# Masking the diagonal blocks of eight forgetting heads on GpSimd instead of TensorE, and preparing the output weight in 32 pieces

## The reference, cut to what matters

```python
def fox_attend(q, k, v, cq, ck, q_pos, k_pos):
    s = jnp.einsum("bqhd,bkhd->bhqk", q, k) * (HEAD_DIM ** -0.5)
    bias = cq[:, :, :, None] - ck[:, :, None, :]        # c: running sum of log f
    mask = k_pos[None, :] <= q_pos[:, None]
    p = jax.nn.softmax(jnp.where(mask, s + bias, -jnp.inf), axis=-1)
    return jnp.einsum("bhqk,bkhd->bqhd", p, v)
# merge: the two normalised, gated groups side by side, times w_out
y = jnp.einsum("bte,ed->btd", jnp.concatenate([ya, yb], -1), w_out)
```

## Time and profile before

| what | value |
|---|---|
| median of 3 runs | 1066.63 us |
| the profiled execution's own time | 1068.08 us |
| its span | 1066.3 us |
| PE busy | 1017.2 us (95%) |
| DVE busy | 661.0 us (62%) |
| ACT busy | 463.4 us (43%) |
| POOL busy | 257.4 us (24%) |

### The profile page before, as it was taken

The page is one execution under the profiler, slowest core; times in us unless marked ns, Lnnn a source line. Parts: engine busy times, 40 slices in busy tenths (PEclk is TensorE's granted clock), DMA queues, the critical chain, the costliest instruction groups (busy, mean ns, idle before and its releaser), DMA issues.

```text
span 1066.3 us, 27354 instructions
## 1 busy us (share of the span) xinstructions
PE 1017.2 (95%) x11316; PEld 858.2 (80%) x11316; DVE 661.0 (62%) x979; ACT 463.4 (43%) x911; POOL 257.4 (24%) x198
## 2 busy tenths in 40 slices
PE   6899999999999999999999998999988999999997
PEld 5898778986778888888878987777766788887886
DVE  5557455654565546565645723676767877787487
ACT  5522312222021232232222323676687787787353
POOL 2300000000000010111201110400065566667596
PEclk9999999999999999999999999999998999999999
DMA  6366787798889787779878787855444452421343
GB/s 228 109 242 230 241 325 290 259 362 317 306 319 353 289 312 284 300 261 369 318 297 299 267 250 232 232 137 130 111 94 93 96 110 60 98 70 51 138 164 133
DMA packets 121328, 234.02 MB, mean 219 GB/s; under 512 B 60536, under 2 KB 91256, under 8 KB 103808
## 3 DMA queue, kind: packets, MB, share of 16 engines
q1 hardware_dynamic: 95872, 209.33, 58.1%
q10 hardware_dynamic: 25344, 23.08, 6.3%
HBM read 204.52 MB, written 27.86 MB: 218 GB/s over the span
## 4 chain that ended last, share of the span: by engine, by line
PE 80%; DVE 5%; issue 4%; ACT 4%; POOL 3%; DMA 2%; ACTq 1%; DVEq 0%; SPq 0%; POOLq 0%
PE bank L887 28%; PE bank L874 8%; PE bank L951 7%; PE bank L997 6%; PE bank L1246 6%; PE bank L1665 6%; PE bank L1222 5%; PE bank L1199 5%; PE bank L980 3%; DVE pr L1468 2%; PE bank L1261 1%; PE bank L1177 1%; DMA k_buf<-in_cache_sb_k 1%; PE bank L940 1%; POOL o_nat L1834 1%
## 5 line engine op out<-in xcount | busy, mean ns | idle before, releaser
L887 PE MATMUL bank<-w_hi,hT_hi 128*128 128x256 f32 (+1 forms) x896 | 260.7, 291 | 3.5 <-DVE hT_lo L620 3.1
L887 PE MATMUL bank<-w_lo,hT_hi 128*128 128x256 f32 (+1 forms) x896 | 253.2, 283 | 0.2 <-issue 0.2
L887 PE MATMUL bank<-w_hi,hT_lo 128*128 128x256 f32 (+1 forms) x896 | 252.9, 282 | 0.0
L887 PEld LDWEIGHTS bank<-w_hi,hT_hi 128*128 128x128 f32 x896 | 170.6, 190 | 11.1 <-issue 5.4
L887 PEld LDWEIGHTS bank<-w_lo,hT_hi 128*128 128x128 f32 x896 | 170.8, 191 | 0.5 <-issue 0.4
L887 PEld LDWEIGHTS bank<-w_hi,hT_lo 128*128 128x128 f32 x896 | 170.6, 190 | 0.0
L534 ACT ACTIVATE u_out<-bank 128x256 f32<-128x256 f32 x112 | 42.9, 383 | 273.7 <-PE bank L887 273.5
L730 DVE STREAM_TRANSPOSE k_buf<-k_buf 128x2048 f32<-128x2048 f32 x64 | 145.4, 2292 | 7.8 <-DMA k_buf<-in_cache_sb_k 7.0
L1478 DVE TENSOR_TENSOR_SCAN om<-om 128x1024 f32<-128x1024 f32 (+3 forms) x64 | 110.0, 1721 | 17.0 <-ACT om L1382 16.3
L1546 POOL TENSOR_TENSOR pr<-pr,om 128x1023 f32<-128x1023 f32 (+3 forms) x64 | 93.3, 1463 | 72.5 <-DVE om L1478 68.7
L1222 PE MATMUL bank<-ident,pr 128*128 128x128 f32 x576 | 87.8, 280 | 9.9 <-POOL pr L1546 4.6
(11 more groups left out here) (203 smaller groups left out, 1931.3 us busy)
## 6 DMA issues: line engine op xcount, KB each, us to landing
k_buf<-in_cache_fox_k SPq DMA_DIRECT2D x32, 1024.0 KB, 9.4
v_ring<-in_cache_fox_v SPq DMA_DIRECT2D x32, 1024.0 KB, 6.8
k_buf<-in_cache_sb_k SPq DMA_DIRECT2D x32, 1024.0 KB, 9.2
v_ring<-in_cache_sb_v SPq DMA_DIRECT2D x32, 1024.0 KB, 6.6
w_raw<-in_w_in SPq DMA_DIRECT2D x14, 1024.0 KB, 8.7
out<-u_out ACTq DMA_DIRECT2D x72, 128.0 KB, 5.3
q_scratch<-u_out ACTq DMA_DIRECT2D x64, 128.0 KB, 5.5
k_nat<-out SPq DMA_DIRECT2D x32, 256.0 KB, 3.9
```

Of the source, the lines that this page charges most:

```text
L887: mm = pe.matmul(bank[:, U + i % 2, w_cols(c)], a[:, k, hcols(s)], b[c % 2][:, k, w_cols(c)], start=(k == 0 and n == 0), stop=(k == KD - 1 ...
```

## The change

Three things. The scores of forgetting heads end without the mask matmul; those of stick-breaking heads keep it. GpSimd instead writes -2^100 above the diagonal of the 128 x 128 block of `c_b` that belongs to a unit, in place, before DVE adds that block. A unit's block is an unmasked column range of the earlier, longer units of the same head, so GpSimd has to wait until the unit before has been moved, and DVE has to wait for GpSimd (`c_hidden`). And the output weight's gains and low parts are made in 16 pieces of 128 x 512 each, put behind those mask writes: the gains from unit 8 on (heads 1 and 2), the low parts from unit 52 on (heads 6 and 7, the last four behind head 7).

```diff
-                    diagonal = seg == i // 4
+                    diagonal = seg == i // 4 and g
...
                     if diagonal:
-                        mm = pe.matmul(out[:, w - P:w], identb[:], mask[g][:], start=False, stop=True,
+                        mm = pe.matmul(out[:, w - P:w], identb[:], mask[1][:], start=False, stop=True,
                                        skip_group_check=True)
...
                 wait_unit_free(dve, p, hh, u)
+                dve.wait_ge(c_hidden, k + 1)
                 plain_wait(dve, sc_ready, k + 1)
...
         def pool_prompt(pool):
-            split_wo(pool)
+            pool.wait_ge(gn_loaded, 32)
+            for h in range(NHEAD // 2):
+                for u in range(NU):
+                    hide_ahead(pool, h, u)
+                    j = NU * h + u
+                    if 0 <= j - SPLIT_AT < 2 * KD:
+                        scale_wo(pool, j - SPLIT_AT)
+                    if 0 <= j - LOWS_AT < 2 * KD:
+                        lower_wo(pool, j - LOWS_AT)
+            for j in range(NU * NHEAD // 2 - LOWS_AT, 2 * KD):
+                lower_wo(pool, j)
...
+        SPLIT_AT, LOWS_AT = NU, NU * (NHEAD // 2 - 2) + 4
+
+        def hide_ahead(pool, h, u):
+            hh, i = h % 2, TP - 1 - u
+            if u == 0:
+                pool.wait_ge(cb_loaded[hh], 16 * (h // 2 + 1))
+            else:
+                pool.wait_ge(s_moved, NU * h + u)
+            x = c_b[:, hh, i * P:i * P + P]
+            pool.affine_select(out=x, in_=x, compare_op=ALU.is_ge, fill=MASKED, base=0,
+                               pattern=[[-1, P]], channel_multiplier=1).then_inc(c_hidden, 1)
+
+        def wo_piece(ap, j):
+            return ap[:, j // 2, W * (j % 2):W * (j % 2) + W]
+
+        def scale_wo(pool, j):
+            if j % 4 == 0:
+                pool.wait_ge(wr_loaded[j // 4], 16)
+            gain = gn_col[:, j // 2:j // 2 + 1].to_broadcast([P, W])
+            pool.tensor_tensor(wo_piece(wo_raw, j), wo_piece(wo_raw, j), gain, ALU.mult).then_inc(wog_done, 1)
+
+        def lower_wo(pool, j):
+            pool.wait_ge(wohi_done, j // 2 + 1)
+            pool.tensor_tensor(wo_piece(wo_lo, j), wo_piece(wo_raw, j), wo_piece(wo_hi, j).bitcast(F32), ALU.subtract
+                               ).then_inc(wolo_done, 1)
...
         def round_wo(act, k):
-            act.wait_ge(wog_done, k // 2 + 1)
+            act.wait_ge(wog_done, 2 * k + 2)
```

More of the change, by code:

```diff
@@ L1040, in build @@
         negmax_ready, pf_ready = sem("negmax_ready"), sem("pf_ready")
+        c_hidden = sem("c_hidden")
         sig_step, scan_done, pb_ready = sem("sig_step"), sem("scan_done"), sem("pb_ready")
@@ L1672, in a_product @@
                 pe.wait_ge(yalo_done, s + 1)
-                pe.wait_ge(wolo_done, 2)
+                pe.wait_ge(wolo_done, KD)
             else:
@@ L1797, in b_product @@
                 pe.wait_ge(s_moved, NU * NHEAD)
-                pe.wait_ge(wolo_done, 4)
+                pe.wait_ge(wolo_done, 2 * KD)
             for n, (at, wide) in enumerate(columns_of(r)):
```

## The result

The changed kernel takes 1072.01 us (median of 14 runs, 1069.20 to 1076.41) against 1068.31 us for the kernel before beside it (14 runs, 1063.95 to 1071.42). The ratio is 1.0037, with a 95% interval of 1.0021 to 1.0052: slower, by 2.2 to 5.6 us. 1070.2 was forecast, as 3.6 us more than the 1066.63 of the first three runs of the kernel before. The profiled execution of the changed kernel took 1074.31 us, its span 1072.5.

A forecast was written before the change was run, and what follows sets the result against it. The chain was taken to alternate between TensorE and DVE within each head. Start +2.5, turns +1.5, registers +0.5, masks -2.2, weight -0.4 and clock +1.7 gave +3.6 on 1066.63: 1070.2 us, range 1064.3 to 1073.

The forecast's parts named there:

- Masks: Forgetting heads: four of eight mask matmuls per head lie on the chain at 0.07 us; 2.2 us gained.
- Start: Prompt stage start: GpSimd's selects queue behind its wait for the norm gains, delaying DVE's first sum; 2.5 us cost.
- Turns and register waits: Heads: DVE and GpSimd alternating between directly following units costs 1.5 us; added register waits in the loop cost 0.5.
- Weight: Output weight in pieces: store ahead of head 7 gains 0.76 us, head 8's start loses 0.4; 0.4 gained.
- Clock: Head 0: TensorE's clock falls to half for 3.4 us after the start stall; 1.7 us cost.
- the hole: Head 0: TensorE idle 3.1 us after unit 1's scores until DVE has moved unit 0.
- B: Rival, 30%: the same start stall and other terms without the clock's fall; 1068.5 us.
- C: Rival, 17%: TensorE paces the heads, all 64 masks gain 4.5 us, turns cost nothing; 1063.8 us.
- D: Rival, 8%: pieces delay selects in heads 1, 2, 6, 7; sign over 0.3 us behind accumulator read; 1074.1 us.

The follow-up runs named there:

- e3: Kernel before without the forgetting heads' mask matmuls, nothing masking their diagonal blocks; 1064.45 us, ratio 0.9967.
- e1: Changed kernel with GpSimd's wait for the norm gains moved from its program's head to its first gain piece; 1070.1 us against 1067.79, ratio 1.0017.
- e2: Kernel before with one wait added: DVE's first sum of head 0 waits for the norm gains; 1070.23 us, ratio 1.0016.
- e6: Kernel before with DVE's `c_hidden` wait ahead of every forget sum, the semaphore raised in advance by 64 GpSimd memsets; 1068.24 us, ratio 1.0008.
- e4: Kernel before with the changed kernel's output-weight pieces on GpSimd; masks stay on TensorE, no DVE wait for GpSimd; 1067.49 us, ratio 0.9987.
- a2: The unaltered changed kernel run and profiled a second time; 1072.97 us (8 runs), ratio 1.0048 against the kernel before.
- e7: From e1: GpSimd masks only units 4, 5 and 6, two low pieces moved forward; 1064.58 us, ratio 0.9968, and again 1064.76 us, 0.9977.

## Why the prediction was right, step by step

The direction and the size came out (3.7 measured, 3.6 forecast), and each term has the sign that it was given. Three costs (start, turns, clock) were sized too low and both gains too high.

- *Masks.* -2.2 forecast, -1.81 measured (e3): right in mechanism and, at four matmuls a head, in size for six of the eight heads.
- *Start.* +2.5 forecast, +3.13 and +3.16 measured. The mechanism is shown by e1, which takes it away, and e2, which makes 1.9 us of it alone. The mis-sizing has three parts: the gains' load is issued 0.59 us behind the first scores, not 0.31; it lands in 3.4 us, not 3.2; and DVE starts 0.24 us behind GpSimd's end, where I had allowed 0.04.
- *Turns and register waits.* +1.5 and +0.5 forecast. Measured together: e1's heads against before, less masks and store, 140.90 - 140.40 + 1.81 + 0.71 = 3.0. This is the term most mis-sized. A turn takes 0.57 to 0.62 us, not 0.41: both handovers are slower than in the earlier trace rows, 0.15 and 0.13 to 0.18 us instead of 0.08 and 0.04. The handovers of those rows stand between other operations, at the kernel's start, and this is where the step went wrong. The bound that I gave, 0.14 behind each release, was nearer. The gap before was read rightly but for heads 3 and 5, where it is 0.25 and not 0.33. The register waits are 0.3 (e6), within their bounds.
- *Weight.* -0.4 forecast. The store came back to 0.42 us and gives 0.71 (e4), the queue at head 8 takes 0.6: -0.1. A low piece lasts 1.30 us and not a quarter of 4.63 us, so five end 0.6 us later than I had them.
- *Clock.* +1.7 forecast. The clock fell in head 0 in both profiles of the changed kernel and not in e1's, and head 0 is 2.2 and 2.5 us longer than e1's. That the hole brings the fall is argued, not shown: the fall follows it in two profiles of two, for 6.8 us each time, but falls of 3.4 us also came at the first scores in four of the eleven profiles without such a hole, and e2 made no hole of this size. The hole was as forecast: 658.48 to 662.39, 3.9 us idle, longer than the 3.1 summed by the start's error. The fall lasted 6.8 us, twice the 3.4 that the term was built on and as long as its upper bound allowed. The trace before had both lengths: its second fall took 3.4 us, and its first, which the earlier trace rows show only at its start, lasted until 817.9, 6.8 us (line below). Of the 3.4 us that half speed could lose in 6.8, 2.2 show, since TensorE was not dense under all of it (662.00 to 663.00 above). The mean granted clock over all runs agrees: 0.9907 in the changed kernel (14 runs; 0.9905 in a2, 8 runs), 0.9922 in e1 (12), 0.9935 before (35). That most executions have the fall is argued from this mean, not seen in each.

The end of that first fall in the trace before (columns as in rows 1):

```profile
817.00:818.00 1.00, 1.00 (x8) 1.00 (x7) 0.00 (x0) 0.96 (x3) 1.00 (x2) 0.55 1.02 207
```

Summed from the traces, with a2's profile: 3.2 + 3.0 - 1.8 - 0.7 + 0.6 + 2.4 = 6.7 us. That this is what the prompt stage shows (156.47 - 149.78 = 6.7) proves nothing by itself, since the 3.0 of the turns was taken as what the other terms leave over; the 2.9 us of longer gaps in e1 are the nearest to a check of it. The medians say 3.7 (2.2 to 5.6) and, in a2, 5.1 (3.0 to 7.4). The second holds the sum, the first ends a microsecond short of it. The prompt stage of before repeats (its heads take 140.40, e2's 140.41). What doesn't repeat lies outside the table: from the first product of head 8 to the end of the span the thirteen profiles take 255.9 to 259.0 us, 258.35 before and 256.92 in a2, in no order with the change, and the falls of the clock there last 3.4 us in some and 6.8 in others. A scatter of this size can hide a microsecond or two between profiles and medians; which way it went in the executions that were only timed stays open. So part of the forecast's nearness is luck: its terms, put right, give 6.7, and it was the terms sized too small that brought its 3.6 so near to the 3.7 measured.

Of the rivals, B is the changed kernel without the fall; no profile caught it so, and its fastest run, 1069.2, is the nearest that is known. C is refuted by the trace of e3: removing all masks gives 1.8 and not 4.5. D's sign appeared, but not its cost. Wherever one sum follows the other directly, the select starts within 0.2 us of its release. Behind a piece of the low parts three start later than the 0.3 us that I had named, by 0.44 and 0.52 us at units 3 and 5 of head 6 and 0.33 at unit 5 of head 7; the gaps between the sums there (0.90, 3.63 and 2.10 us) are what they were before.

## What to carry to other kernels

A matmul that costs 0.07 us cannot be replaced at a gain by a round trip between two other engines that costs 0.4 more than going on directly, unless something else already stands between the two halves of that trip: the same edit gains where it is kept to the units with such cover (e7, 0.2 to 0.3% faster than before) and loses where it is not. A wait put at the head of an engine's program holds up everything that is later moved in behind it; when work moves onto an idle queue, read what stands first in it. And a hole in TensorE's work may have a second price behind it, the clock: here 2.2 to 2.5 us in the two profiles that have a hole of 3.9 us or more.

## What was not expected of the hardware

The same operation cut in four is not four quarters: 1.30 us for 128 x 512 against 4.63 for 128 x 2048, and 1.04 against 3.60 for the gains (means of 16 and of 4):

```profile
L1638 POOL TENSOR_TENSOR wo_lo<-wo_raw,wo_hi 128x512 fp32r<-128x512 f32 x16 | 20.5, 1297 | 0.1
```

The pieces take 0.56 us more than the whole, in both: 0.19 us for each of the three instructions that were added. And an instruction of DVE with two inputs in SBUF is held up by the GpSimd instruction that runs: the store of 0.42 us became 1.22 at 809.03 and ended 0.15 us behind the end of a piece, at about 810.1 (the five pieces shared out evenly). One with an input in PSUM, the forget sum itself, keeps its 1.09 us beside a piece (792.76, with GpSimd busy from 792.60).
